# A hybrid decoder step on one core: the copy of the window cache issued later in the DMA queue, and the prompt's weighted rows put in the weights' region and shared out anew

## What is computed

```python
def chunk_partials(kv, pos_w):
    ...
    chunks = kv[:, :nck * CMP_STRIDE].reshape(B, nck, CMP_STRIDE, 2, KV_HEADS, HEAD_DIM)
    pw = pos_w.reshape(2, ratio, CMP_STRIDE, HEAD_DIM)
    return jnp.einsum('bcjsgd,smjd->mbcsgd', chunks, pw)
```

```python
    kw = jnp.concatenate([win_state.astype(kvw.dtype), kvw], axis=1)
    ...
    return combine_nsa(gates, o_c, o_s, o_w), kvc, kvs, kw[:, -w_keep:]
```

## Time and profile before

| what | value |
|---|---|
| median of 3 runs | 1127.68 us (1124.9 to 1129.37) |
| profiled execution, its own time | 1124.82 us |
| its span from the first to the last instruction | 1123.2 us |
| PE busy | 1017.9 us, 91% of the span, 6562 records |
| DVE busy | 592.4 us, 53% |
| ACT busy | 307.9 us, 27% |
| POOL busy | 71.8 us, 6% |
| mean granted clock of PE | 0.946 of full speed |
| DMA moved | 147.79 MB, mean 132 GB/s |

### The profile page before, as it was taken

How to read it: one execution, slowest core, us unless ns; L and a number is a source line. 1 busy time by engine, 2 the same in 40 slices (tenths; PEclk the granted TensorE clock), 3 DMA queues, 4 the chain that set the end, 5 groups by cost and what they waited for, 6 DMA issues and landing times.

```text
span 1123.2 us, 17593 instructions
## 1 busy us (share of the span) xinstructions
PE 1017.9 (91%) x6562; PEld 626.6 (56%) x6562; DVE 592.4 (53%) x1330; ACT 307.9 (27%) x749; POOL 71.8 (6%) x124
## 2 busy tenths in 40 slices
PE   6999999999779999599999997768999799999897
PEld 3567676776544454377565465445555565664443
DVE  3207879776346554999000005348886466656113
ACT  4310000000330231011102114236777443533101
POOL 0000000000000000000000005030000112110000
PEclk9999999999889999799999997768999999999899
DMA  8623565353514366654222102430001857865202
GB/s 323 219 60 124 160 188 158 91 162 115 190 39 112 113 243 233 179 155 127 75 75 75 38 1 76 139 102 1 1 1 56 314 196 267 292 210 174 95 1 84
DMA packets 45727, 147.79 MB, mean 132 GB/s; under 512 B 8393, under 2 KB 20170, under 8 KB 38858
## 3 DMA queue, kind: packets, MB, share of 16 engines
q1 hardware_dynamic: 40522, 129.89, 36.0%
q0 software_dynamic: 5120, 16.78, 4.3%
HBM read 139.63 MB, written 15.27 MB: 138 GB/s over the span
## 4 chain that ended last, share of the span: by engine, by line
PE 71%; DVE 13%; DMA 7%; ACT 4%; issue 4%; SPq 1%; POOL 1%; POOLq 0%; DVEq 0%; ACTq 0%
PE PS L1181 62%; PE PS L1184 10%; DMA arena<-in_ccmp 3%; DVE arena L1811 2%; DVE arena L1812 2%; DVE arena L2074 1%; DMA arena<-in_csel 1%; DMA arena<-in_cmem 1%; DMA arena<-in_wall 1%; DVE arena L2093 1%; ACT arena L1156 1%; ACT arena L1130 1%; DVE arena L1814 1%; DVE arena L1901 1%; DVE arena L1779 1%
## 5 line engine op out<-in xcount | busy, mean ns | idle before, releaser
L1181 PE MATMUL PS<-arena 128*32 128x64 f32 (+18 forms) x5468 | 863.0, 385 | 46.0 <-DVE arena L1822 12.8
L1181 PEld LDWEIGHTS PS<-arena 128*128 128x128 f32 (+6 forms) x5468 | 499.4, 153 | 386.7 <-issue 247.5
L1184 PE MATMUL PS<-arena 128*128 128x128 f32 (+3 forms) x1094 | 172.5, 299 | 51.8 <-ACT arena L831 10.9
L1184 PEld LDWEIGHTS PS<-arena 128*128 128x128 f32 (+3 forms) x1094 | 128.4, 151 | 101.8 <-issue 40.5
L1811 DVE TENSOR_TENSOR arena<-arena 128x2048 f32<-128x2048 f32 x32 | 73.3, 2290 | 20.4 <-DMA arena<-in_ccmp 19.2
L2010 DVE SCALAR_TENSOR_TENSOR arena<-arena 128x576 f32<-128x576 f32 x8 | 5.8, 757 | 129.6 <-ACT arena L1004 129.4
L1812 DVE TENSOR_TENSOR arena<-arena 128x2048 f32<-128x2048 f32 x32 | 73.2, 2286 | 0.0
L1085 ACT ACTIVATE arena<-arena 128x512 f32<-128x512 f32 (+3 forms) x96 | 52.9, 554 | 21.6 <-DVE arena L2074 21.6
L2074 DVE CUSTOM_DVE_ANT_0 arena<-PS,arena 128x512 f32<-128x512 f32 (+3 forms) x96 | 41.5, 488 | 20.0 <-PE PS L1181 20.0
L537 POOL DMA_DIRECT2D arena<-in_csel x64 | 34.5, 539 | 237.3 <-PE PS L1184 112.6
L1970 DVE TENSOR_TENSOR arena<-arena,PS 128x512 f32<-128x512 f32 x16 | 11.0, 688 | 58.9 <-PE PS L1181 58.9
(11 more groups left out here) (184 smaller groups left out, 551.2 us busy)
## 6 DMA issues: line engine op xcount, KB each, us to landing
arena<-in_wall SPq DMA_DIRECT2D x20, 2048.0 KB, 9.3
arena<-in_ccmp SPq DMA_DIRECT2D x128, 256.0 KB, 3.7
arena<-in_csel SPq DMA_DIRECT2D x64, 256.0 KB, 5.6
arena<-in_csel POOLq DMA_DIRECT2D x64, 256.0 KB, 6.0
arena<-in_cmem SPq DMA_DIRECT2D x32, 256.0 KB, 3.6
arena<-in_win SPq DMA_DIRECT2D x8, 1024.0 KB, 10.0
out_win_s<-in_win SPq DMA_DIRECT2D x1, 8064.0 KB
arena<-in_xp SPq DMA_DIRECT2D x1, 2048.0 KB, 16.9
```

The costliest lines, as they stand in the source:

```text
L1181: return nc.tensor.matmul(out, lhsT, rhs, start=start, stop=stop, skip_group_check=True)
L1184: return nc.tensor.transpose(out, in_, ident[0:in_.shape[0], 0:in_.shape[0]])
```

## The change

The copy of the window cache is taken out of SP's program between the pages of tile 21 and the gate weights, and put behind the prompt's stores, ahead of the 36 loads of the gates. `PA` and `PB` are placed at offsets 0 to 4095, the region of `W[0]`, in which at that time only finished data of the memory attention lie. Their multiplications no longer wait for `r_turned`, only for `ms_done` and `roped` (the rotation of queries and keys, long done). DVE makes `PA` and the last two of `PB`, POOL the first two of `PB`; PE's wait counts this.

```diff
-        PA = [at(10240 + 512 * n, 512) for n in range(4)]
-        PB = [at(o, 512) for o in (8192, 8704, 12288, 12800)]
+        PA = [at(512 * n, 512) for n in range(4)]
+        PB = [at(2048 + 512 * n, 512) for n in range(4)]
...
             load_pages(CONV_TILES + 4, CONV_TILES + OUT0_TILES + 2)
-            sp.dma_start(O["win_s"][:, 0:WIN - NT, :], I["win"][:, NT:WIN, :]).then_inc(win_copied, 16)
             sp.dma_start(Wg.rearrange("p k c -> p (k c)"), I["wg"]).then_inc(wg_in, 16)
...
+            sp.dma_start(O["win_s"][:, 0:WIN - NT, :], I["win"][:, NT:WIN, :]).then_inc(win_copied, 16)
             sp.wait_ge(gates_written, 16)
             sp.wait_ge(qz_zero, 2)
...
             pool.wait_ge(ms_done, 2)
             pool.wait_ge(roped, 4)
-            pool.wait_ge(r_turned, 11)
-            for p in range(PT):
+            for p in range(2):
...
-            pe.wait_ge(cp_ra, NB * NTL + PT)
-            pe.wait_ge(cp_rb, NB * NTL + PT)
+            pe.wait_ge(cp_ra, NB * NTL + PT + 2)
+            pe.wait_ge(cp_rb, NB * NTL + 2)
...
+            dve.wait_ge(ms_done, 2)
+            dve.wait_ge(roped, 4)
+            for rows, name, tiles in ((PA, "pos0", range(PT)), (PB, "pos1", range(2, PT))):
+                for p in tiles:
+                    tt(heads(rows[p][:, 0:256]), heads(P1[2][:, p, 256:512]), row_pos(name, 0), ALU.mult)
+                    tt(heads(rows[p][:, 256:512]), heads(P1[3][:, p, 0:256]), row_pos(name, 1), ALU.mult).then_inc(cp_ra, 1)
             dve.wait_ge(qz_zero, 2)
             dve.wait_ge(r_turned, 11)
-            for p in range(PT):
-                tt(heads(PA[p][:, 0:256]), heads(P1[2][:, p, 256:512]), row_pos("pos0", 0), ALU.mult)
-                tt(heads(PA[p][:, 256:512]), heads(P1[3][:, p, 0:256]), row_pos("pos0", 1), ALU.mult).then_inc(cp_ra, 1)
```

## The result

The median of 3 runs is 1094.32 us (1089.35 to 1094.85), against 1127.68 us (1124.9 to 1129.37) of the kernel before: a ratio of 0.969 with a 95% interval of 0.964 to 0.975. The change makes the kernel 33 us faster by these medians.

The account below looks back on a forecast made before the run. PE was taken to bound the kernel (71% of the chain), with waits behind the copy and for POOL. 17.9 + 7.0 = 24.9 us off 1124.8 gives 1099.9, plus 2.9 for the runs' median: 1102.8 us, range 1097 to 1110.

Parts of the forecast that it names:

- Part 1: Layer 1 projections: moving the copy away removes late weights and pages (DVE waits 17.11 us for tile 22), gaining 17.9 us.
- the three of PE: PE waits in layer 1 projections: 2.43 us for weights, 12.08 for tile 23's rows, 0.69 for tile 29's.
- The margins: Projections without the copy: how far DVE's tiles are ready ahead of PE; closest is tile 29, 1.2 us.
- Part 2: Prompt's weighted rows begun with the transposes: 6.1 us of wait gone, with clock effects 3.9 to 7.9, taken as 7.0.
- up to 2.2: Steps from the prompt's sums to the scores may get the lower clock, costing up to 2.2 us more.
- Part 3: Copy in its new place behind the prompt's stores: costs nothing, between 0 and 1 us.
- The conversion to the runs: End of the sum: 2.9 us added to 1099.9, as the runs' median stood above the profiled execution.
- The page tiles: Rival, projections: late pages bind DVE instead; part 1 gives 12 us, time 1108.7; chance 0.08.
- The early rows: Rival, weighted rows: they bring no more than their start, 3.9 us or a little less, 1105.9 to 1107; chance 0.10.
- Instructions: Rival, prompt's attention: the copy holds up instruction fetches, 1129.8 to 1144.8 us; chance 0.05, 0.03 counted as slower.
- The stores: Rival: the prompt's stores land with the copy, so mask and scores wait 35.6 us, 1138.4 us; chance 0.02.
- The copy was not hidden: Negates the rival that the copy was hidden anyway in the projections, part 1 empty, 1120.7 us; chance 0.02.

Follow-up runs that it names:

- the runs of the copy alone: Kernel before with only the window copy moved behind the stores, weighted rows as before: 1107.18 us, ratio 0.984 (0.981 to 0.988).
- The runs of place and shares: Changed kernel with old place and twelve-four shares: 1105.01 us in one execution; with new place and eight-eight shares: 1090.9 us, ratio 0.974.
- the shares alone: Changed kernel with weighted rows back in their old place and the wait for `r_turned`, shares twelve and four kept: 1105.01 us in one execution.
- the run with even shares: Changed kernel with DVE and POOL making eight multiplications each in the new place: 1090.9 us, ratio 0.974 (0.970 to 0.977).
- the run with DVE late: Changed kernel with two buffer clears (128 x 2048) on DVE ahead of tile 22's products: 1098.43 us in one execution.

## Why the prediction was right in kind and 8.5 us off

Two terms of the sum failed: the 2.9 us of the conversion from the profiled execution to the runs, which later runs do not show, and the clock in part 2, sized too small. What the two parts do, and part 1's size, came out as predicted.

- **Part 1, 17.9 us: right**, in its size and its steps. The stretch lost 18.0 us, and the runs of the copy alone show 17.5 (13 to 22). The wait of DVE, the three of PE and the 2.7 us of lower clock are gone, and nothing stepped in their place. The margins came out as worked out: tile 29 is ready at 494.8, PE's sums of it start at 496.08, 1.3 us later where I had 1.2; tile 23 had 2.7 where I had 2.6 (452.0 less 449.4).
- **Part 2, the 6.1 us of wait: right.** Everything is done 5.9 us after DVE's start, as worked out, and the sums follow ACT's last copy at once. The runs of place and shares confirm that the place gives it.
- **Part 2, the clock: mis-sized**, in "I take 7.0". I gave the sums half of their possible gain and bounded the part at 7.9. The sums won 1.72 us (3.65 to 1.93), as the upper bound had it; the loss of "up to 2.2" in the steps behind them didn't come, 4.67 us before and 4.69 after. (The loss does occur, and is 1.7 us at most here: at a granted clock of 0.50, in the runs of the copy alone and of the shares alone, the steps take 6.39 us, and at 0.72, in the second profile of the change, 5.36.) Part 2 is 8.5 us by the means of three profiles each, 9.8 by the pair of the result, above my upper bound. Of the 9.8, 7.4 lie up to the end of the sums, 0.6 in the first eight matmuls of the scores (3.36 to 2.78) and 1.8 behind them (10.34 to 8.49), where two other profiles with the old rows had 8.50 and 8.58. So that last piece isn't shown to be the change's.
- **Part 3, nothing: right**, by the runs without and with two copies. The mask didn't wait for the stores (in the run with even shares it did, for 0.5 us). That SP would stand in the gate loads I had missed; it had time.
- **The conversion to the runs: failed.** "The median of the runs stands 2.9 us above that execution" was added as if it belonged to the kernel. Later runs do not bear it out: eleven others have their median at 1124.16 and seven more at 1122.34, both below the profiled 1124.82. So it was the scatter of three runs, or of the occasion. Without it the forecast is 1099.9. The range's lower end took 2.8 us for the spread of the runs, from three runs within 4.5; eleven runs span 14.0.

The 8.5 us add up: 2.9 of that offset, 5.1 by which the profiled executions differ more (29.97 against 24.9: 2.9 ahead of 407 us, which is not the change's, 2.8 of part 2, 0.1 of part 1, less 0.7 elsewhere), and 0.5 by which after's profiled execution lies above its median. Some of the miss is the measurement's: by the longer comparison the change gives 28.4 us (24 to 33), in which 24.9 still has its place, near the edge.

**The rivals.** The page tiles did not bind; the run with DVE late shows how near they are. The early rows brought more, not less, than their start. Instructions were not held up: the prompt's attention takes the same time with and without the copy. But in 715 to 762 us the instruction queue moved two packets beside the copy, as few as in the earlier trace rows, so this was hardly put to the test:

```profile
q8 instruction: 2, 0.03, 0.3%
```

The stores landed ahead of the copy (the last step of `kv_stored` is at 715.24), and the run that puts them behind it shows what that would have cost, by SP's standing and by slow landing. The copy was not hidden before.

What stays open is why the clock of the memory attention of layer 0 differs from one execution to the next, and what decides whether SP stands behind a copy. Neither was tried.

## What to carry to other kernels

Find the long transfer that nobody waits for, and look at what is queued behind it: put it where everything with a deadline has already been issued ahead of it, and what follows has slack for its whole length, the issuing engine's own time included. Where two engines slow each other down and a third waits for both, look first at why they start so late: here another place in memory brought 6 us, and other shares half of one. A forecast from one profiled execution goes against the median of many runs; here an offset taken from three was gone in the next eleven, and the spread of three was no bound.

## What the runs showed of the hardware that was not expected

- SP can stand in the issue of a DMA while a long copy is in its queue: 37.19 us in the fourth DMA behind it, and 50.76 us for 36 loads of 0.2 KB that take 14.01 without the copy. A DMA that is issued behind a long one can hold up SP's whole program, not just its own data. It need not: in the old place ten DMAs behind the copy took SP at most 0.40 us each.
- The same copy of 8064 KB lands 27.9 us after its issue with a slowest dimension of 16, and 42.8 with one of 8; its semaphore rises in sixteen steps at the end in the one case, in eight in the other. Of stores issued behind it with one of 8, half of the semaphore's steps came within 5 us and half only when the copy was through.
- The same 328 matmuls of the same kernel (layer 0's memory attention, which has short waits all along) took 40.4 us at a granted clock of 0.90 in one execution and 43.4 at 0.80 in another; the runs of the kernel before span 14 us.
